# One 512-column matmul for both parts of the activations in a 2x2 product scheme with seven products, with sums seeded in PSUM

## The reference

```
h = rmsnorm(x, g_ffn)                    # 512 x 2048
a = einsum('tkd,td->tk', u_sel, xs)      # u_sel: chosen rows of expert_u
hid = gelu(a, approximate=False) * g     # g: softmax of the 16 best scores of each head
out = einsum('tk,tkd->td', hid, expert_v[idx])
```

## Time and profile before

| what | value |
|---|---|
| median of 3 runs | 4242.04 us (4237.77 to 4245.73) |
| profiled execution, its own time | 4239.96 us |
| its span | 4238.2 us |
| PE busy | 4162.4 us (98%) |
| DVE busy | 2666.0 us (63%) |
| ACT busy | 1564.0 us (37%) |
| POOL busy | 2491.5 us (59%) |
| mean granted TensorE clock | 0.995 of full speed |
| first matmul of the first pair, first one behind the last pair | 2158.01 and 3199.04 us |

### The profile page before, as it was taken

How to read it: one execution, slowest core, us unless ns; L and a number is a source line. 1 busy time by engine, 2 the same in 40 slices (tenths; PEclk the granted TensorE clock), 3 DMA queues, 4 the chain that set the end, 5 groups by cost and what they waited for, 6 DMA issues and landing times.

```text
span 4238.2 us, 67530 instructions
## 1 busy us (share of the span) xinstructions
PE 4162.4 (98%) x24972; PEld 3799.8 (90%) x24972; DVE 2666.0 (63%) x3758; ACT 1564.0 (37%) x2079; POOL 2491.5 (59%) x1295
## 2 busy tenths in 40 slices
PE   7999999999999999999999999999999999999998
PEld 7888888888887878888899999999999999999998
DVE  5422443355436442799467777777776887888786
ACT  5222333333334432322344444444443333333333
POOL 5333344344443444444578888888206888888873
PEclk9999999999999999999999999999999999999999
DMA  7696566666666875223345555555438999999994
GB/s 253 201 386 184 156 207 188 192 185 192 185 191 216 272 232 166 82 89 122 119 120 134 124 137 129 131 131 132 135 131 295 361 369 364 358 372 370 366 376 143
DMA packets 579978, 900.01 MB, mean 212 GB/s; under 512 B 87344, under 2 KB 425696, under 8 KB 558704
## 3 DMA queue, kind: packets, MB, share of 16 engines
q1 hardware_dynamic: 404768, 597.10, 43.8%
q0 software_dynamic: 83584, 168.19, 13.7%
q10 hardware_dynamic: 91472, 132.69, 8.8%
HBM read 813.98 MB, written 218.09 MB: 244 GB/s over the span
## 4 chain that ended last, share of the span: by engine, by line
PE 61%; POOL 14%; issue 13%; DVE 5%; DMA 4%; ACT 1%; ACTq 1%; DVEq 0%; POOLq 0%; SPq 0%
PE banks L2191 13%; PE banks L2193 13%; PE banks L2192 13%; PE banks L2528 6%; PE banks L2529 6%; PE banks L2527 6%; POOL w_lo L841 6%; POOL w_lo L770 4%; DMA arena<-expert_rows_scratch,constants 2%; POOL constants L822 2%; POOL arena L834 2%; DMA w_raw<-w_u 1%; PE banks L2392 1%; DVE w_lo L2015 1%; DVE banks L2084 1%
## 5 line engine op out<-in xcount | busy, mean ns | idle before, releaser
L2191 PE MATMUL banks<-x_hi,w_hi 128*128 128x512 f32 (+1 forms) x4800 | 1753.4, 365 | 34.3 <-POOL w_lo L841 13.2
L2192 PE MATMUL banks<-x_lo,w_hi 128*128 128x512 f32 (+2 forms) x4928 | 1772.8, 360 | 0.0
L2193 PE MATMUL banks<-x_hi,w_lo 128*128 128x512 f32 (+1 forms) x4800 | 1735.2, 362 | 0.0
L770 POOL TENSOR_TENSOR w_lo<-w_raw,w_hi 128x1024 fp32r<-128x1024 f32 x364 | 901.7, 2480 | 1412.8 <-ACT w_hi L855 1216.1
L2191 PEld LDWEIGHTS banks<-x_hi,w_hi 128*128 128x128 f32 x4800 | 903.5, 188 | 154.7 <-issue 19.6
L2192 PEld LDWEIGHTS banks<-x_lo,w_hi 128*128 128x128 f32 x4928 | 930.6, 189 | 105.0 <-issue 1.2
L2193 PEld LDWEIGHTS banks<-x_hi,w_lo 128*128 128x128 f32 x4800 | 903.6, 188 | 108.9
L855 ACT ACTIVATE w_hi<-w_raw 128x1024 fp32r<-128x1024 f32 x612 | 642.8, 1057 | 953.4 <-PE banks L2193 744.5
L793 POOL DMA_INDIRECT gate_matrix_scratch<-arena,constants x384 | 741.5, 1931 | 116.8 <-issue 116.8
L841 POOL TENSOR_TENSOR w_lo<-w_raw,w_hi 128x1024 fp32r<-128x1024 f32 x203 | 492.6, 2431 | 82.0 <-ACT w_hi L855 78.0
L2529 PE MATMUL banks<-x_hi,w_lo 128*128 128x256 f32 x1664 | 470.8, 283 | 0.0
(11 more groups left out here) (309 smaller groups left out, 4685.9 us busy)
## 6 DMA issues: line engine op xcount, KB each, us to landing
expert_rows_scratch<-w_v SPq DMA_DIRECT2D x256, 512.0 KB, 5.2
w_raw<-w_u SPq DMA_DIRECT2D x256, 512.0 KB
w_raw<-w_v SPq DMA_DIRECT2D x256, 512.0 KB
w_raw<-w_in SPq DMA_DIRECT2D x200, 512.0 KB
gelu_scratch<-arena ACTq DMA_DIRECT2D x126, 256.0 KB
gate_matrix_scratch<-early_mix_or_one_hots SPq DMA_DIRECT2D x16, 1536.0 KB, 9.3
constants<-gelu_scratch ACTq DMA_DIRECT2D x128, 176.0 KB
early_mix_or_one_hots<-gate_matrix_scratch ACTq DMA_DIRECT2D x30, 704.0 KB
```

Source lines behind the costliest of these rows:

```text
L770: nc.gpsimd.tensor_tensor(wlo[s][:], raw[s][:], whi[s][:], ALU.subtract).then_inc(w_lo_made, 1)
L2191: M.matmul(out, whi[s][:, k], h, start=f, stop=False)
L2192: M.matmul(out, whi[s][:, k], l, start=False, stop=False)
L2193: ins = M.matmul(out, wlo[s][:, k], h, start=False, stop=e)
```

## The change

The high and low part of the activations now lie in one tensor (`x_split`, and for t1, t2, t4 the `_split` ones), so that one matmul with high weights streams both, 256 columns of each, into the two halves of a PSUM bank. The low weights times the high activations go into the first half. A product is thus 8 matmuls of 512 columns and 8 of 256, in place of 24 of 256. The sum of the two halves is taken when a bank is read.

The sums of products are now made in PSUM. Each pair has four banks, a, b, c, d (`PAIR_BANKS`, two sets by turns). `11` goes into a, then ACT copies a to b, and the products `s2`, `s3` and `22` are accumulated on b and `12` on a; after `s2` ACT copies b to c, where `s4` is added. `s1` goes to d, which ACT copies to SBUF (`shared_parts`). DVE reads a quarter with an addition over both halves (TENSOR_REDUCE), or an addition of 512 columns and then one of 256. The order of the products, and with it that of the operands and sums on ACT and DVE, changes as `SEVEN` says. Two matmuls of 512 columns ahead of the first pair write banks 4 and 5 once.

```diff
-SEVEN = ["11", "s2", "12", "s3", "s1", "22", "s4"]
+SEVEN = ["11", "s1", "s2", "12", "s3", "s4", "22"]
+PAIR_BANKS = [(2, 0, 1, 3), (6, 4, 5, 7)]
...
-        xhi = sb("x_hi", [P, KT, T], F32R)
-        xlo = sb("x_lo", [P, KT, T], F32R)
+        x_split = sb("x_split", [P, 2, KT, T], F32R)
+        xhi, xlo = x_split[:, 0], x_split[:, 1]
...
-            operand_t[n] = [nc.alloc_sbuf_tensor_at(f"{n}_{part}", [P, HT, TH], F32R,
-                                                    offset=arena_at + 4 * (a.at + k * HT * TH))
-                            for k, part in enumerate(("hi", "lo"))]
+            operand_t[n] = nc.alloc_sbuf_tensor_at(f"{n}_split", [P, 2, HT, TH], F32R, offset=arena_at + 4 * a.at)
...
-                    sp.wait_ge(pair_lo, 7 * i + 6)
+                    sp.wait_ge(pair_lo, 7 * i + 7)
...
+                a, b, c, d = PAIR_BANKS[u % 2]
                 def done(j):
                     act.wait_ge(pair_done, 28 * i + (7 * u + j))
                 def result(j):
-                    act.wait_ge(pair_out, 16 * i + (4 * (u + 1) + j))
...
+                    act.wait_ge(pair_out, 24 * i + (6 * (u + 2) + j))
+                def gelu(v):
+                    A.activation(v, v, ACT.Gelu).then_inc(pair_gelu, 1)
+                def copy(into, of):
+                    A.activation(into, bank[of][:], ACT.Copy).then_inc(pair_copied, 1)
                 following = (i + 1, 0) if u == 3 else (i, u + 1)
                 done(1)
-                act.wait_ge(pair_out, 16 * i + (4 * u + 1))
-                A.activation(first_product, bank[4][:, 0:TH], ACT.Copy).then_inc(pair_copied, 1)
-                operand_hi(i, u, "s1")
+                copy(bank[b][:], a)
+                operand_hi(i, u, "s3")
+                done(2)
+                copy(shared_parts.rearrange("p z t -> p (z t)"), d)
+                operand_hi(i, u, "s4")
+                done(3)
+                copy(bank[c][:], b)
                 operand_hi(i, u, "22")
-                operand_hi(i, u, "s4")
-                result(1)
-                act.wait_ge(gelu_out[0], 64 * i + 16 * (PAIRS_FROM // 2 + u) + 16)
-                gelu(quads[:, 0, 0], z6_c11[:, 1])
...
+                else:
+                    operand_hi(*following, "11")
+                result(1)
+                gelu(quads[:, 0, 0])
...
+                    operand_hi(*following, "s1")
+                result(3)
+                gelu(quads[:, 1, 1])
...
                     operand_hi(*following, "s2")
...
                     operand_hi(*following, "12")
...
+                result(6)
+                gelu(eg.rearrange("p a b -> p (a b)")[:, TH:3 * TH])
                 act.wait_ge(pair_gelu, 12 * i + (3 * (u + 1) + 3))
...
-            def pair(i, u, last=False, between=lambda: None):
+            def pair(i, u, last=False):
+                a, b, c, _ = (bank[n][:].rearrange("p (z t) -> p z t", z=2) for n in PAIR_BANKS[u % 2])
                 def done(j):
                     dve.wait_ge(pair_done, 28 * i + (7 * u + j))
                 def result(j):
-                    dve.wait_ge(pair_out, 16 * i + (4 * (u + 1) + j))
...
+                    dve.wait_ge(pair_out, 24 * i + (6 * (u + 2) + j))
...
+                def add(out, x, y_):
+                    V.tensor_tensor(out, x, y_, ALU.add).then_inc(pair_out, 1)
+                def add_halves(out, banks):
+                    V.reduce_sum(out, banks.rearrange("p z t -> p t z"), AX_X).then_inc(pair_out, 1)
+                def c12():
+                    done(6)
+                    add(shared_parts, shared_parts, c)
+                    result(4)
+                    add(quads[:, 0, 1], shared_parts[:, 0], shared_parts[:, 1])
                 following = (i + 1, 0) if u == 3 else (i, u + 1)
-                operand_lo(i, u, "s1")
                 weight_sum(i, u, 4)
+                operand_lo(i, u, "s3")
+                operand_lo(i, u, "s4")
                 operand_lo(i, u, "22")
-                done(3)
-                dve.wait_ge(pair_copied, 4 * i + (u + 2))
-                dve.wait_ge(pair_gelu, 12 * i + (3 * u + 1))
-                add(z6_c11, first_product.unsqueeze(1).broadcast_to([P, 2, TH]), both(5))
-                operand_lo(i, u, "s4")
                 if last:
                     dve.sem_inc(w_lo_made, 4 * PAIRS)
-                    between()
+                    for k in range(4):
+                        product(0, k)
+                done(4)
+                stored(0)
+                add_halves(quads[:, 0, 0], a)
+                if not last:
+                    operand_lo(*following, "11")
+                done(5)
+                dve.wait_ge(pair_copied, 12 * i + (3 * u + 2))
+                add(c22_parts, shared_parts, b)
+                stored(1)
+                result(2)
+                add(quads[:, 1, 1], c22_parts[:, 0], c22_parts[:, 1])
+                if last:
+                    low_part(0, 0, 0)
+                    for k in range(1, 5):
+                        low_part(0, k, 0)
+                        product(0, k + 3)
+                    c12()
+                    for k in range(5, 8):
+                        low_part(0, k, 0)
                 else:
-                    operand_lo(*following, "11")
                     weight_sum(*following, 1)
                     weight_sum(*following, 2)
-                done(5)
-                result(1)
-                add(z75, z6_c11[:, 0:1].broadcast_to([P, 2, TH]), both(6))
-                stored(1)
-                result(2)
-                add(quads[:, 1, 1], z75[:, 0], bank[6][:, TH:T])
+                    operand_lo(*following, "s1")
+                    c12()
+                    operand_lo(*following, "s2")
+                    weight_sum(*following, 3)
+                done(7)
+                add_halves(quads[:, 1, 0], b)
                 if not last:
-                    weight_sum(*following, 3)
-                    operand_lo(*following, "s2")
                     operand_lo(*following, "12")
...
+            for n in PAIR_BANKS[1][1:3]:
+                M.matmul(bank[n][:], xhi[:, KT - 1, 0:P], xhi[:, KT - 1], start=True, stop=True)
+            def product_of(i, u, name, into, k0, b0, split=x_split, fresh=False):
                 pe.wait_ge(pair_lo, operand_number(i, u + 1, name))
                 s = operand_slot(u, name)
                 cols = slice(b0, b0 + TH)
+                first_half = bank[into][:, 0:TH]
+                both = bank[into][:].rearrange("p (z t) -> p z t", z=2)
                 for k in range(HT):
-                    h, l = his[:, k0 + k, cols], los[:, k0 + k, cols]
-                    M.matmul(out, whi[s][:, k], h, start=k == 0, stop=False)
-                    M.matmul(out, whi[s][:, k], l, start=False, stop=False)
-                    ins = M.matmul(out, wlo[s][:, k], h, start=False, stop=k == HT - 1)
+                    M.matmul(both, whi[s][:, k], split[:, :, k0 + k, cols], start=fresh and k == 0, stop=False,
+                             skip_group_check=True)
+                    ins = M.matmul(first_half, wlo[s][:, k], split[:, 0, k0 + k, cols], start=False, stop=k == HT - 1,
+                                   skip_group_check=True)
                 ins.then_inc(pair_done, 1)
             def pair(i, u):
-                def result(j):
-                    pe.wait_ge(pair_out, 16 * i + (4 * u + j))
-                pe.wait_ge(pair_copied, 4 * i + (u + 1))
-                product_of(i, u, "11", bank[4][:, 0:TH], 0, 0)
+                a, b, c, d = PAIR_BANKS[u % 2]
+                def copied(j):
+                    pe.wait_ge(pair_copied, 12 * i + (3 * u + j))
+                pe.wait_ge(pair_out, 24 * i + (6 * u + 6))
+                product_of(i, u, "11", a, 0, 0, fresh=True)
+                pe.wait_ge(t_lo, 1)
+                product_of(i, u, "s1", d, 0, 0, operand_t["t1"], fresh=True)
                 pe.wait_ge(t_lo, 2)
-                result(1)
-                product_of(i, u, "s2", bank[5][:, 0:TH], 0, 0, *operand_t["t2"])
-                product_of(i, u, "12", bank[5][:, TH:T], HT, 0)
+                copied(1)
+                product_of(i, u, "s2", b, 0, 0, operand_t["t2"])
+                product_of(i, u, "12", a, HT, 0)
                 pe.wait_ge(t_lo, 5)
-                result(3)
-                product_of(i, u, "s3", bank[6][:, 0:TH], 0, TH)
-                product_of(i, u, "s1", bank[6][:, TH:T], 0, 0, *operand_t["t1"])
-                result(4)
-                product_of(i, u, "22", bank[7][:, 0:TH], 0, 0, *operand_t["t4"])
-                product_of(i, u, "s4", bank[7][:, TH:T], HT, TH)
+                copied(3)
+                product_of(i, u, "s3", b, 0, TH)
+                product_of(i, u, "s4", c, HT, TH)
+                pe.wait_ge(pair_out, 24 * i + (6 * (u + 2) + 2))
+                product_of(i, u, "22", b, 0, 0, operand_t["t4"])
```

80 lines of the change are left out of this document (29 added, 51 removed).

## The result

The changed kernel takes 4269.45 us in the median of 4 runs (4266.31 to 4274.75); the kernel before, run beside it, 4243.88. The ratio is 1.0066, with a 95% interval from 1.0053 to 1.0079: slower, by 0.5 to 0.8%. The prediction was 4262, with a range from 4234 to 4293. The profiled execution took 4270.1 us.

A forecast was written before the change was run, and what follows sets the result against it. PE alone set the pace before; after, a chain through DVE and ACT makes PE wait at `s2`, 20.34 us a pair. 51 intervals (1037.3) plus 4.2 and the ends give 1061.4 against 1041.0: +20, so 4262 us, range 4234 to 4293.

The forecast's parts named there:

- The chain: From one start of `s2` to the next, through PE, DVE, ACT and the copy a to b: 20.34 us a pair.
- restart of PE: At `s2`, PE starts again with an empty pipeline, so the second matmul comes later than usual: 0.10 us a pair.
- a sign of being wrong: PE standing less than 0.7 us in a pair, through stores or a reduction on the chain faster than taken.
- step 1: On PE, the products `s2`, `12` and `s3` at 2.76 us each: 8.28 us a pair.
- The rival that put 12 ns more on a two-block matmul: 24 such matmuls in the chain each cost 12 ns more: 0.29 us a pair, 4277 us; chance 8%.
- the rival that took the extra time away: Alternating wide and narrow matmuls on PE cuts their extra 12 to 13 ns to 2 to 3: 4237 us; chance 2%.
- the 0.35 at each loop's end: ACT's copy comes 0.35 us late at the end of a loop's body, now holding PE: 12 times, 4.2 us.
- The end of the stage: Behind the last pair, PE's waits for low parts of the activations stay unchanged; 2 us would be the most.
- The load of `22`: Weight block for DVE's weight sum 1 arrives at 9.5 to 9.9 us, wanted at 9.7: a tie, no wait taken.
- The rival at 4286 to 4293: The load of `22` is late by 0.6 us a pair for 40 to 51 pairs: 24 to 31 us more; chance 14%.
- PE is never held up: PE waits nowhere in the pairs and the change saves its full 36 us: 4206 us; chance 13%.
- no change: In the pairs, chain and old period differ by 0.1 us at most: 4242 us; chance 13%.

The follow-up runs named there:

- the first of these kernels: The changed kernel, with ACT's copy of bank a to b for the next pair moved ahead of this pair's last GELU and two stores; 4226.58 us.

## Why the prediction was right, and where its sum was short

**The chain.** Its steps as forecast and as the trace after has them:

| step | forecast | after |
|---|---|---|
| start of `s2` to DVE's first addition: three products and 0.38 | 8.66 | 2615.86 to 2624.68: 8.82 |
| DVE's block, with the reduction | 8.62 | 2604.26 to 2612.90: 8.64 |
| GELU, stores, until the copy starts | 2.31 | 2612.90 to 2615.15: 2.25 |
| copy, until PE goes on | 0.65 | 2615.15 to 2615.86: 0.71 |
| restart of PE | 0.10 | 0.10, part of the first row |
| a pair | 20.34 | 20.42 |

The reduction into 256 columns costs what its 512 inputs cost (0.68). The copy into PSUM costs what it did from SBUF (0.58), and PE goes on 0.13 behind its end where 0.06 was taken. PE stands at `s2` alone, and nothing waits ahead of `s3` or `22`. The stand was forecast as 1.0 us with the restart and is 0.8 (20.42 less 19.62), because PE's own period is 19.62 and not 19.32. Without the restart it is 0.66, just below the 0.7 that the prediction named as a sign of being wrong; but that sign was for faster stores or a faster reduction, and these cost what was taken (1.31 and 0.68).

**The mis-sized term** is step 1, three products at 2.76. The price of 0.226 for a wide matmul came from another stage; here it is 0.231 to 0.232. A product is 19.62/7 = 2.80. The three on the chain took 8.43 (2615.86 to the start of `s4` at 2624.39, less the restart) in place of 8.28. Of these 0.15 us DVE's start 0.29 behind the end of `s3`, where 0.38 was taken, gave 0.09 back, so that the first row of the table hides part of the error. The same error takes off nearly half of what a kernel without the wait could win: 0.39 a pair is left of 0.70. The rival that put 12 ns more on a two-block matmul had the sign right and the size and reason wrong, since one block costs the same. The Trainium skill ("TensorE: Matmul & The Clock Gate", section Back-to-back issue gap) gives columns/2.4 + 2.5 ns for matmuls by themselves at full clock. Here each matmul has its own weight load, and what comes on top of the columns is 12 to 13 ns and some 18 for the wide ones in the pairs (0.231 less 0.213), so the trace doesn't agree, and the rival that took the extra time away falls.

**The term that was missing** is ACT's queue at the loop's exit. The sum had 51 equal intervals and the 0.35 at each loop's end, which the trace confirms (20.76 and 20.45 in place of 20.42: 0.37 in all). It didn't follow the chain through the code between the loop and the last pairs, though the kernel shows four DMA issues there, the issue of two stores was already in the sum at 1.31, and the interval at the exit was already 21.99 before. That is 4.2 us of the 8.1 by which the stage is over the forecast (1069.5 against 1061.4; 24.93 where 20.34 + 0.35 was counted). The other 50 intervals give 50 x 0.08 = 4.0, the last two of them, 20.14 and 20.11, give back 0.6, and the loop's ends and the first and last products make up the rest. The move of the loads shows the part of the exit.

**The end of the stage** was taken as unchanged. In the trace after PE waits there for the low parts of the activations for 1.20 us, for 0.35 and, at 3234.11, for 1.41, where before it waited for 1.48, 0.35 and 0.34, and the granted clock falls, where before it stayed at 1.00. After, the last of these starts and the window, and behind them the window before:

```profile
3234.11 0.66 PE L2208 MATMUL banks<-x_split,w_hi 128*128 128x352 f32 x1 [1.41 <-DVE x_split L2115]
3232.00:3237.00 5.00, 3.59 (x13) 3.31 (x14) 3.44 (x7) 2.15 (x3) 2.33 (x1) 0.68 1.03 373
```

```profile
3200.00:3205.00 5.00, 2.82 (x15) 1.96 (x14) 4.73 (x8) 1.59 (x4) 1.26 (x1) 1.00 0.96 344
```

The waits are 0.8 us longer in all. From the third on, the next twelve matmuls take 3.45 us (3234.11 to 3237.56) where they took 2.03 before (3204.32 to 3206.35), which is 1.4 us for the clock. Of these 2.2 us only 1.1 are left at the end of the span. What made the clock fall is not shown, and the stand alone is not enough: before, one of 1.48 us left it at 1.00, and in the kernel with the copy ahead of the stores waits of 0.94, 0.35 and 1.40 us at the same place did too (1.00 from 3185 to 3195).

**The load of `22`**, forecast as a tie, is no wait: DVE's block begins on PE's release and runs through, also in the kernels with a period of 19.6. The rival at 4286 to 4293 falls. So do *PE is never held up* and *no change*, by the 0.66 us in each pair. The first of them is what the change could be: with one instruction placed otherwise PE is never held up, and the time is not 4206 but 4219 to 4227, since the width is worth less than taken and the exit stays long (22.64 in the first of these kernels).

## What to carry to other kernels

- Sums seeded in a bank turn a copy that nobody was waiting for into one that PE waits for. Follow the queue of the engine that makes the copy back from it, and put the copy ahead of everything that doesn't need to come first, above all stores: their issue holds the engine too (0.65 us each here).
- A chain that runs once per iteration has also to be followed through the loop's end and through the code behind the loop. A burst of DMA issues that is harmless beside the work can be a whole stand there.
- The price of an instruction taken from another stage was 2% off; times 56 in a pair, this took nearly half of what the edit could win.

## What was unexpected of the hardware

- 512-column matmuls of the same form take 0.226 us each in the stage before and 0.231 to 0.232 in the pairs. A plain range, a plain output and grouping by width changed nothing. The cause is open.
- After a stand of 3.61 us PE went on with the granted clock at half. In the kernel with the added copy on the chain, with stands of 1.86 to 2.15 us at the ends of the loop's body, it fell at 4 of 11, 1.4 us after PE had gone on in the one shown; at the other 7 the stands were as long and it stayed at 1.00. After the stands of 0.66 us of the changed kernel, and its stands of about 1.0 us at the ends of the loop's body, it never fell: windows of 5 us from 2160 to 3150 all read 1.00.
- ACT's four loads of 176 KB took 2.98 us to issue in one row (2.52 and 3.50 at the same place in two other kernels), and 0.36 + 1.41 when they were moved to where ACT had other work between them. An issue has no fixed price; why it was less there was not tried.
